# State space scan group by group, with a second stream of projections and Fourier products between its parts

## What is computed

```
p = h @ w_in                                  # x, B, C, step sizes, z, f, gate_f, gate_s
y = scan(x, dt, B, C) both ways + d_skip * x  # 4 groups of 8 heads, chunks of 128 tokens
y_ssd = rmsnorm(y * silu(z), w) @ w_ssd_out
u = fft2(f, tokens and 128 channels).real
y_four = u @ w_four_out
mix = (sigmoid(gate_f) * y_four + sigmoid(gate_s) * y_ssd) @ w_o
```

## Time and profile before

| what | value |
|---|---|
| median of three runs | 3232.49 us |
| profiled execution | 3232.91 us |
| its span, first to last instruction | 3231.3 us |
| mean granted PE clock | 0.957 of full speed |
| PE busy / weight loads | 2991.0 us (93%) / 1603.5 us |
| DVE, ACT, POOL busy | 1119.7, 483.4, 544.1 us |
| mean DMA rate over the span | 224 GB/s |

### The profile page before, as it was taken

The page is one execution under the profiler, slowest core; times in us unless marked ns, Lnnn a source line. Parts: engine busy times, 40 slices in busy tenths (PEclk is TensorE's granted clock), DMA queues, the critical chain, the costliest instruction groups (busy, mean ns, idle before and its releaser), DMA issues.

```text
span 3231.3 us, 39368 instructions
## 1 busy us (share of the span) xinstructions
PE 2991.0 (93%) x16166; PEld 1603.5 (50%) x16166; DVE 1119.7 (35%) x1859; ACT 483.4 (15%) x847; POOL 544.1 (17%) x650
## 2 busy tenths in 40 slices
PE   5998788998799999999999988998999999799996
PEld 2446453857333333333333326877887778433333
DVE  3665562011333333333333323463001446222112
ACT  1111111001110111101010102233001232211111
POOL 0000650000122323232323211021110011000000
PEclk9998788999799999999999999999999999799998
DMA  6344002324299999999999973122443211599991
GB/s 226 116 145 160 1 1 104 129 102 160 108 375 395 396 395 397 394 397 394 397 394 397 395 292 127 53 79 87 145 143 128 105 38 43 186 387 385 386 386 67
DMA packets 334385, 728.08 MB, mean 225 GB/s; under 512 B 17920, under 2 KB 63420, under 8 KB 333932
## 3 DMA queue, kind: packets, MB, share of 16 engines
q1 hardware_dynamic: 321456, 697.22, 58.3%
q0 software_dynamic: 8896, 24.59, 2.1%
q10 hardware_dynamic: 3836, 3.58, 0.4%
HBM read 708.55 MB, written 16.78 MB: 224 GB/s over the span
## 4 chain that ended last, share of the span: by engine, by line
PE 67%; DVE 2%; DMA 2%; ACT 1%; issue 1%; SPq 0%; POOL 0%; POOLq 0%; ACTq 0%; DVEq 0%; PEldq 0%
PE P L705 65%; PE P L708 2%; DVE R L1597 1%; DMA WS<-in_w_gate_up 1%; ACT R L2304 0%; ACT L2304 0%; SPq L626 0%; DMA R<-expert_rows,small 0%; ACT xT L2304 0%; DMA expert_rows<-R 0%; ACT ea L2304 0%; POOL R L2826 0%; DVE R L2295 0%; DVE xT L1603 0%; DVE R L1603 0%
## 5 line engine op out<-in xcount | busy, mean ns | idle before, releaser
L705 PE MATMUL P<-R 128*32 128x512 f32 (+10 forms) x6484 | 1264.4, 493 | 88.0 <-POOL R L2668 30.9
L705 PE MATMUL P<-WS,R 128*64 128x512 f32 (+4 forms) x4456 | 1007.4, 589 | 9.5 <-POOLq L2737 2.8
L705 PEld LDWEIGHTS P<-R 128*32 128x32 f32 (+4 forms) x6484 | 525.6, 145 | 551.5 <-issue 461.7
L705 PEld LDWEIGHTS P<-WS,R 128*64 128x64 f32 (+2 forms) x4456 | 314.7, 129 | 633.7 <-issue 620.2
L2304 ACT ACTIVATE R<-P 128x512 f32<-128x512 f32 (+6 forms) x432 | 224.5, 521 | 2001.7 <-PE P L705 1691.5
L705 PE MATMUL P<-R,WS 128*128 128x256 f32 (+1 forms) x1888 | 504.7, 427 | 10.5 <-DVE R L1600 3.5
L1597 DVE TENSOR_TENSOR R<-P,R 64x512 f32<-64x512 f32 (+3 forms) x260 | 171.8, 661 | 781.9 <-ACT R L2304 478.0
L705 PEld LDWEIGHTS P<-R,WS 128*128 128x128 f32 x1888 | 357.6, 191 | 144.2 <-issue 98.4
L705 PE MATMUL P<-xT,WS 128*128 128x256 f32 (+2 forms) x1728 | 401.1, 385 | 9.5 <-ACT xT L2304 3.5
L705 PEld LDWEIGHTS P<-xT,WS 128*128 128x128 f32 (+2 forms) x1728 | 318.0, 188 | 70.9 <-issue 21.3
L1597 DVE TENSOR_TENSOR R<-R 128x512 f32<-128x512 f32 (+9 forms) x360 | 254.8, 708 | 64.9 <-ACT R L2304 53.0
(11 more groups left out here) (163 smaller groups left out, 985.6 us busy)
## 6 DMA issues: line engine op xcount, KB each, us to landing
WS<-in_w_gate_up SPq DMA_DIRECT2D x192, 1024.0 KB, 11.3
R<-in_w_down SPq DMA_DIRECT2D x128, 1024.0 KB, 12.9
R<-in_w_gate_up SPq DMA_DIRECT2D x64, 1024.0 KB, 14.4
WS<-in_w_in SPq DMA_DIRECT2D x60, 1024.0 KB, 7.5
WS<-in_w_mod SPq DMA_DIRECT2D x24, 1024.0 KB, 7.4
R<-in_moe_w_down SPq DMA_DIRECT2D x23, 1024.0 KB, 8.6
WS<-in_moe_w_gate SPq DMA_DIRECT2D x20, 1024.0 KB, 11.2
WS<-in_moe_w_down SPq DMA_DIRECT2D x17, 1024.0 KB, 8.2
```

The lines of the kernel that those rows point to most:

```text
L705: return nc.tensor.matmul(out, lhsT, rhs, start=start, stop=stop, skip_group_check=True)
```

## The change

The gs, u, z, ff1, ff2 and gf products become one list of 40 items and 256 products (`FRONT`), cut into parts (`PARTS1`); PE's `front(name)` issues a part. Parts stand behind the step sizes, behind the second and fourth decay sum, in each of the 32 scan steps and behind the scan. They use banks P2 and P3 in turn, with semaphores f_done and f_free; ACT empties them, DVE those of z. The scan runs group by group: four steps, both directions in each. `decays` of the next step now stands before the front part in every step, ahead of dg. The products of z with Y (`gate_y`) stand in DVE's queue behind the fourth and sixth step of a group, for the group before. Buffers move: GS into the context half of hT, V_ and UT into x tiles of finished groups, zs and YT into BT, GF into Bf and Cf, U and MX into the place that H left. POOL's Y_init waits for x's transposes only, so it runs in the convolution stage. The transposes of Y come in two halves, before the first and second w_ssd_out unit. The order of weight units follows. Left out below are the removed stage code, index changes of H and the old ACT loops.

```diff
+FRONT = ([("gs", m) for m in range(8)] + [("u", i) for i in range(4)] + [("z", 0), ("z", 1)]
+         + [("f1", f) for f in range(4)] + [("z", 2), ("z", 3)] + [("f1", f) for f in range(4, 8)]
+         + [("z", 4), ("z", 5)] + [("f2", i) for i in range(4)] + [("z", 6), ("z", 7)] + [("gf", m) for m in range(8)])
+FRONT_MM = [(j, k) for j, (kind, _) in enumerate(FRONT) for k in range({"f1": 2, "f2": 4}.get(kind, 8))]
+PARTS1 = ([("dt", 24), ("seg1", 8), ("seg3", 12)]
+          + [((g, q), k) for g, ks in enumerate(([10, 10, 5, 5, 5, 5, 6, 6], [3] * 8, [3] * 8, [3] * 6 + [7, 7]))
+             for q, k in enumerate(ks)]
+          + [("end1", 16), ("end2", 8), ("end3", 56)])
+PART1, _at = {}, 0
+for _n, _k in PARTS1:
+    PART1[_n] = (_at, _at + _k)
+    _at += _k
...
+        zt = reg(SCR, 2, N)
+        zs = [BT[:, :, 512 * i:512 * i + 128] for i in range(2)]
+        YT = reg(12288, 16, N)
+        GS = hT[:, :, 0:N]
+        GF = [Bf[:, t, :] for t in (0, 1, 2, 4, 5, 6)] + [Cf[:, t, :] for t in range(2)]
+        MX = reg(24576, KT, N)
+        U = reg(26624, 2, D)
+        V_ = [XT[:, f % 4, 512 * (f // 4):512 * (f // 4) + 512] for f in range(8)]
+        UT = [XT[:, i, 1024:1536] for i in range(4)]
...
-                  + [proj(w_in, OFF_Z + 512 * i, 512) for i in range(4)]
-                  + [down(a["w_ssd_out"][0], 4 * i, 4) for i in range(4)]
                   + [proj(w_in, OFF_GS + 512 * i, 512) for i in range(2)]
                   + [proj(w_in, OFF_F + 512 * i, 512) for i in range(2)]
+                  + [proj(w_in, OFF_Z + 512 * i, 512) for i in range(4)]
                   + [proj(w_in, OFF_GF + 512 * i, 512) for i in range(2)]
+                  + [down(a["w_ssd_out"][0], 4 * i, 4) for i in range(4)]
                   + [proj(a["w_four_out"][0], 512 * i, 512) for i in range(2)]
                   + [proj(a["w_o"][0], 512 * i, 512) for i in range(2)])
...
-        SSD = [(d, step, ((0, 1, 2, 3), (1, 0, 3, 2))[d][step], g) for d in range(2) for step in range(4) for g in range(4)]
+        SSD = [(d, step, ((0, 1, 2, 3), (1, 0, 3, 2))[d][step], g) for g in range(4) for step in range(4) for d in range(2)]
+        STATES = [(d, step, g) for d, step, c, g in SSD if step < 3]
...
                     unit_used()
                     mod_unit(4 + j // 4)
+            fu = [0]
+            def front(name):
+                for q in range(*PART1[name]):
+                    j, k = FRONT_MM[q]
+                    kind, i = FRONT[j]
+                    if k == 0:
+                        if kind in ("gs", "gf") and i % 4 == 0 or kind in ("u", "z") and i % 2 == 0:
+                            fu[0] = unit()
+                        if j >= 2:
+                            pe.wait_ge(S("f_free"), j - 1)
+                    if k == 1 and j and (FRONT[j - 1][0] in ("gs", "gf") and FRONT[j - 1][1] % 4 == 3
+                                         or FRONT[j - 1][0] in ("u", "z") and FRONT[j - 1][1] % 2 == 1):
+                        pe.wait_ge(S("f_done"), j)
+                        pe.sem_inc(S("unit_used"), 1)
+                    b = P[2 + j % 2]
+                    if kind in ("gs", "gf"):
+                        last = mm(b[:, 0:N], wproj(fu[0], 512, k, 128 * (i % 4), 128 * (i % 4) + 128), hT[:, k, N:2 * N],
+                                  k == 0, k == 7)
+                        end = k == 7
+                    elif kind in ("u", "z"):
+                        c = N + 128 * (i % 2)
+                        last = mm(b[:, :], hT[:, k, c:c + 128], wproj(fu[0], 512, k, 0, 512), k == 0, k == 7)
+                        end = k == 7
+                    elif kind == "f1":
+                        last = mm(b[:, :], U[:, k, 128 * i:128 * i + 128], k1("dft")[:, 512 * k:512 * k + 512], k == 0, k == 1)
+                        end = k == 1
+                    else:
+                        h, t = k // 2, k % 2
+                        last = mm(b[:, 256 * h:256 * h + 256], k1(("dfc", "dfs")[t]), V_[2 * i + h][:, 256 * t:256 * t + 256],
+                                  t == 0, t == 1)
+                        end = k == 3
+                    if end:
+                        last.then_inc(S("f_done"), 1)
+                    if q == len(FRONT_MM) - 1:
+                        pe.wait_ge(S("f_done"), len(FRONT))
+                        pe.sem_inc(S("unit_used"), 1)
             n = unit()
             turn_mod(11)
             b = job("dt", 0)
...
                               k == 0, k == KT - 1)
             done(last)
             unit_used()
+            front("dt")
             pe.wait_ge(S("dA_ready"), 1)
             for c in range(4):
@@ -891,6 +950,8 @@
                     mm(b[:, 64 * q:64 * q + 32], k1(f), dA[:, c, 0:32])
                     last = mm(b[:, 64 * q + 32:64 * q + 64], k1(r), dA[:, c, 32:64])
                 done(last)
+                if c % 2:
+                    front(f"seg{c}")
...
+                if i + 1 < len(SSD) and SSD[i + 1][1] >= 2:
+                    decays(i + 1, nx + 1 if step >= 2 else nx)
+                front((g, i % 8))
                 if step >= 2:
-                    if i + 1 < len(SSD) and SSD[i + 1][1] >= 2:
-                        decays(i + 1, nx + 1)
...
+            for name in ("end1", "end2", "end3"):
+                front(name)
+            pe.wait_ge(S("dg_used"), nx)
+            pe.wait_ge(S("f_free"), len(FRONT))
+            pe.wait_ge(S("mix_step"), 1)
+            for u in range(4):
+                if u < 2:
+                    for i in range(4 * u, 4 * u + 4):
...
+                pe.wait_ge(S("mm_free"), START["ytr"] + 2 * (u + 1))
...
+            eight("four", lambda k: UT[k // 2][:, N * (k % 2):N * (k % 2) + N])
...
             dve.wait_ge(S("Y_init"), 2)
-            for d, step, c, g in SSD:
+            def gate_y(i):
+                g, c, j = i // 2, i % 2, FRONT.index(("z", i))
+                b, four = P[2 + j % 2][:, :].rearrange("p (q n) -> p q n", q=4), zs[i % 2]
+                dve.wait_ge(S("z_sig"), i + 1)
+                tt(four, four, b).then_inc(S("f_free"), 1)
+                dve.wait_ge(S("f_free"), j + 1)
+                yc = Y[:, c, 512 * g:512 * g + 512].rearrange("p (q n) -> p q n", q=4)
+                mark(tt(yc, yc, four), "z_used")
+            for i, (d, step, c, g) in enumerate(SSD):
                 hs = slice(32 * d + 8 * g, 32 * d + 8 * g + 8)
                 yg = Y[:, c - 2, 512 * g:512 * g + 512] if step >= 2 else None
                 if step >= 2:
...
-                F(n, tt(zs[:, i % 2, :], zs[:, i % 2, :], b[:, :]))
-                yc = Y[:, c, 512 * u:512 * u + 512]
-                mark(tt(yc, yc, zs[:, i % 2, :]), "z_used")
+                if g and i % 8 in (3, 5):
+                    gate_y(2 * (g - 1) + (i % 8 == 5))
+            gate_y(6)
+            gate_y(7)
             rooted()
             V(ts(Y[:, 0, :], Y[:, 0, :], st[:, 0:1], None, ALU.mult, ALU.bypass))
             mark(ts(Y[:, 1, :], Y[:, 1, :], st[:, 1:2], None, ALU.mult, ALU.bypass), "mix_step")
...
+            fj = [0]
+            def front(name):
+                q = PART1[name][1]
+                while fj[0] < len(FRONT) and (q == len(FRONT_MM) or FRONT_MM[q][0] > fj[0]):
+                    j = fj[0]
+                    kind, i = FRONT[j]
+                    b = P[2 + j % 2]
+                    fj[0] += 1
+                    act_.wait_ge(S("f_done"), j + 1)
+                    if kind == "z":
+                        if i >= 2:
+                            act_.wait_ge(S("z_used"), i - 1)
+                        mark(fn(zs[i % 2], b[:, :].rearrange("p (q n) -> p q n", q=4), ACT.Sigmoid), "z_sig")
+                        continue
+                    wait(act_, "f_free", j)
+                    if kind == "gs":
+                        ins = fn(GS[:, i, :], b[:, 0:N], ACT.Sigmoid)
+                    elif kind == "gf":
+                        ins = fn(GF[i], b[:, 0:N], ACT.Sigmoid)
+                    elif kind == "u":
+                        ins = fn(U[:, i % 2, 512 * (i // 2):512 * (i // 2) + 512], b[:, :], ACT.Copy)
+                    else:
+                        ins = fn((V_ if kind == "f1" else UT)[i], b[:, :], ACT.Copy)
+                    ins.then_inc(S("f_free"), 1)
+                    act_.wait_ge(S("f_free"), j + 1)
...
+            front("dt")
+                if c % 2:
+                    front(f"seg{c}")
+            nx = 0
+            for i, (d, step, c, g) in enumerate(SSD):
+                if i + 1 < len(SSD) and SSD[i + 1][1] >= 2:
+                    act_.wait_ge(S("seg_done"), nx + 1)
+                    if nx:
+                        act_.wait_ge(S("MT_ready"), nx)
+                    A(fn(EX[:, 0:512], P[5][:, :], ACT.Exp))
+                    mark(fn(EX[:, 512:1024], P[6][:, :], ACT.Exp), "EX_ready")
+                    nx += 1
+                front((g, i % 8))
+
+            front("end1")
+            front("end2")
+            front("end3")
...
```

(34 more changed lines are left out.)

89 lines of the change are left out of this document (15 added, 74 removed).

## The result

The changed kernel takes 3143.57 us (median of 4 runs, 3141.0 to 3146.0) where the kernel before, in the same session, takes 3231.37 (3226.64 to 3234.87): a ratio of 0.9729, 95% interval 0.9712 to 0.9746, some 88 us less. The forecast was 3161, its range 3143 to 3195. The profiled execution took 3141.0 us, its span 3139.4.

A forecast was written before the change was run, and what follows sets the result against it. PE, busy 93% of 3231.3 us, was taken as the bound. Starting w_four_out at 661.7 instead of 735.4 us, less 2.0 for Y_init, saves 71.7: 3232.9 becomes 3161 us, range 3143 to 3195.

The forecast's parts named there:

- step 7: Transposes and w_ssd_out units behind the gf units: 63.5 us, so the w_four_out product starts at 661.7 us.
- step 8: Y_init in the convolution: two POOL products may delay DVE by 0 to 6 us, taken as 2.
- Steps 1 to 3: Step sizes' end (308.9) to scan start (340.2 us): gs matmuls 12.5 and 8.8, decay sums 8.0, half clock 2.0.
- Step 4: PE work in the scan: output steps 89.0, state products alone 14.0, front matmuls 99.7, sum 202.7 us.
- Step 5: Cover in the scan: no other engine is the bound; uncovered waits cost 8.0 us, weight loads at seams 2.
- Step 6: Behind the scan: z6 and z7 14.0 us, then gf units hiding the norm's root 31.3, PE idling 2.6.
- it goes better: Rival, chance 0.09: the uncertain 8.0, seams, clock, Y_init and 2.2 of the sums vanish; 3145 us.
- The holes stay open: Rival, chance 0.12: state product handshakes are paid at all 24 later-group steps, 30 to 42 us; 3191 to 3203.
- Clock: Rival, chance 0.04: many short waits at the seams keep PE at half clock through the scan; 3364 us.
- No effect: Rival, chance 0.03: a load or semaphore order holds the w_four_out product or the experts; 3233 us.

The follow-up runs named there:

- yinit_dt: The changed kernel with POOL's Y_init waiting for the end of the convolution, so it runs under the step size projection; 3141.84 us, ratio 0.9716.
- gate_cb: The changed kernel with the second gate product of a group issued after CBm of the seventh step; 3141.09 us, ratio 0.971.
- lumped: The changed kernel with the same front matmuls given to the scan in blocks rather than three per step; 3196.9 us, ratio 0.9891.
- yinit_late: The changed kernel with POOL's Y_init back behind the decay factors, as before the change; 3157.19 us, one run.
- best: The changed kernel with the edits of yinit_dt and gate_cb, and the square of Y's first half ahead of z7's sigmoid; 3135.64 us, ratio 0.9697.
- gate_early: The changed kernel with the gate product issued before DVE's wait for PE's diagonal part, ahead of the Y addition; 3143.1 us, ratio 0.9716.

## Why the prediction was right, and where its sizes were off

The mechanism was the forecast's: the holes of the state passes, the decay chain and the root take the front matmuls, the clock stays up, and what is left is one wait per group for CBm and one for the root. The time came out 20.2 us lower than forecast (3141.0 against 3161.2, profiled execution to forecast). Of this, 15.2 lie before the w_four_out product (663.7 us, the 661.7 of step 7 and the 2.0 of step 8, against 648.5) and 5.0 in the unchanged rest, which is within the scatter of the runs above. The median of the runs, 3143.57 us, is 0.6 us above the lower end of the range, 3143, and two of the four runs lie under it: that the time fell inside is luck, and the gain was forecast too small, 72 us for 88. By steps:

- *Steps 1 to 3* (31.3 us): measured 27.3, from 313.8 to 341.1. Two rows of the changed kernel's timeline, PE:

```profile
313.88 13.39 PE L724 MATMUL P<-R,WS 128*128 128x256 f32 x48
327.10 2.76 PE L724 MATMUL P<-small,C 128*128 128x32 f32 x24
```

  The page counts each of these matmuls as two records, so the 24 gs took 13.4 where I said 12.5 (12.1 to 12.4 in yinit_dt, gate_cb, lumped, yinit_late and best). The decay sums were the term that I had mis-sized: 12 of the 24 take 2.76 us at full clock, 5.5 in all against my 8.0, just under my lower bound (5.8). The 2.0 for more half clock was not needed beside the cold start. And the wait of 9.7 us for POOL is gone, as forecast.
- *Step 4* (202.7 us of PE work in the scan): measured 195.0 busy. An output step takes 4.72 us from start to start without a state product (2.64 for the product with H and dg, 2.08 for the next decay products), and so 5.58 with one, where I put 5.20 and 5.92. The step of 5.20 held its own gap of 0.31 us and the tail of the matmul ahead of it, 0.16. The step of 5.92 held no idle time and was at clock 1.00, yet 22 merged records of it took 0.4 us longer than the 22 at the same place of a step take in the changed kernel; no run shows why:

```profile
449.24 4.28 PE L705 MATMUL P<-R 128*128 128x64 f32 x22
424.12 3.89 PE L724 MATMUL P<-R 128*128 128x64 f32 x22
```

  (The first row is of the kernel before.) Eight steps of each are 6.6 us. A unit's duration holds its last matmul's tail, so 0.86 us per 512 columns is right for a seam, not 0.873: some 2 us in 132 front matmuls and the states. Some 1 us goes the other way, for the tails ahead of the eight waits are in the busy time.
- *Step 5* (8.0 us of waits, 2.0 of seams): measured 7.1 us of waits, and nothing at the seams. Three waits for CBm of 1.76 us against 1.7 to 2.1; the waits for POOL in the fifth step 0.3 against 0.4; f2 0.7 against 0.5. gate_early and gate_cb show that the gate product in DVE's queue is what makes PE wait. POOL was 80.6 us busy in the scan, DVE 95.3, ACT 50.3, of 202.1: none is the bound. No seam exposes a weight load.
- *Step 6* (14.0 and 31.3 us): measured 13.8 and 31.1, with an idle time of 2.50 us for ACT where I had 2.6, behind three gf units:

```profile
570.03 17.53 PE L724 MATMUL P<-R,WS 128*128 128x256 f32 x80 [2.50 <-ACT R L2337]
588.14 1.94 PE L727 MATMUL P<-C,R 128*128 128x128 f32 x16 [0.57 <-ACT R L2337]
```

- *Step 7* (63.5 us): measured 60.4. I had taken the transposes at the busy time of the earlier trace rows, which was at clock 0.65. At full clock 16 records take 1.94 us, not 3.0: 2.3 us for both halves. The rest is again the unit's tail.
- *Step 8* (2 us, bounds 0 and 6): measured 4.5 (and 0.4 more, since the step size projection took 14.0 us for 13.6), the one term that went the other way. I thought that POOL's first product would fall into DVE's own wait; it does, for 2.5 of its 3.6 us, but its end holds up DVE's scaling (1.36 us for 0.55), and the second product holds up the first tap product until it is done (3.99 us for 0.8). That makes DVE 4.0 us late, 2.4 more than its slack of 1.6; the other 2 us or so are the half clock behind PE's idle time, which I had left out. The Trainium skill (SBUF — State Buffer, "Who interferes with whom") states an exclusive lock between the two engines; the first tap product, which ends only behind POOL's second product, agrees with it. The step as that rule alone would have it was put at 5.6 us, with the whole 7.2 us of POOL on DVE; the measured 4.5 lies between that and my 2.

The errors of steps 1 to 7 add up to 18.1 us in the same direction (4.0, 10.6, 0.4 and 3.1), less 2.9 of step 8. Most of them have one source: durations read from stretches in which PE was partly at half clock (the sums, the transposes) or had gaps (the output steps), used for a stream in which it has neither. Of the signs that I had named, the clock, the waits and their releasers, and the convolution (4.5 us longer, under the 6) came as said. The sizes did not: the scan with its front takes 202 us and not 213, PE's busy time falls by 38 us and not 20, and POOL and DVE are busy for 40 and 47% of the scan and not 50 to 60.

Of the rivals, *it goes better* (3145) is where the time came out, though not for its reason alone: of the 16.2 us that it took away, the waits (8.0) are nearly all there (7.1) and Y_init cost 2.9 more instead of 2.0 less; only the seams, the sums and the 2.0 for the clock went. The prices of the output steps and the transposes, which it left alone, gave the rest, so that its number fits is mostly luck. *The holes stay open* did not happen with three front products per step; lumped shows it happening, and dearer (54 us in the scan) than the 30 to 42 put down, since the cover works in the output steps too. *Clock*: 1.00 over the whole scan. The Trainium skill (TensorE: Matmul & The Clock Gate, "A second HAM failure mode: psum-queue depth-cycling") tells of a kernel whose clock oscillates from short idle times as it cycles through PSUM banks. The two banks of the front show no such thing here, at clock 1.00; idle times of 1 to 2.5 us in the variants are sometimes followed by a single drop. *No effect*: excluded, w_four_out starts 86.9 us earlier.

What stays open: how the gain divides between the places outside the scan (no run has the front there alone), why a step with a state product is 0.4 us shorter now, the price of Y_init's old place in the new kernel (one run, mixed with other drops of the clock), and why the same idle time is sometimes followed by half clock and sometimes not.

## What to carry to other kernels

When a chain of short products with handshakes cannot be made faster, put independent long work into every one of its gaps; here three matmuls of 512 columns at a time were enough, and the same work in blocks kept only 35 us of the 88. Price a dense stream from start to start of neighbours in a full clock stretch, not from a stage's busy time or a unit's duration. And ask of each operation moved to "idle" POOL which DVE instructions it will lie beside: under the step sizes, where DVE has next to nothing to do, these two products cost nothing that the profile shows; in the convolution they cost 4.5 us.

## What was not expected of the hardware

A short idle time of PE can cost more than itself. The granted clock fell to half for some 3 to 4 us behind idles of 1.07 us (best), 1.75 (yinit_dt), 1.76 (yinit_late, twice), 1.97 (gate_early), 2.34 (the convolution of the changed kernel) and 2.50 us (gate_cb). Behind the same idle times it also stayed full: behind 1.07 us in gate_cb, behind 1.76 us three times and 2.50 us once in the changed kernel. The windows of yinit_late behind its wait of 5.16 us, and of best behind 1.07 us, show the drop:

```profile
343.50:347.50 4.00, 4.00 (x8) 2.52 (x9) 0.69 (x1) 0.00 (x0) 1.04 (x1) 0.50 0.00 0
```

```profile
529.00:533.00 4.00, 4.00 (x21) 2.92 (x21) 1.60 (x3) 0.39 (x1) 1.04 (x1) 0.74 0.00 0
```

A drop costs 1 to 2 us here, some 3 behind the wait of 5.16 us. These runs show no rule for when it comes, and it is one reason why the sum of small waits removed is not quite the time gained.

A POOL product of two SBUF tensors can hold up a single DVE operation for nearly its whole length: the first tap product took 3.99 us instead of 0.8 beside a POOL product of 3.68, and the three behind it were not slowed. DVE's multiplication by a per-partition scalar, with one tensor in SBUF as its input, is held up too, in the one place seen: 1.36 us instead of 0.55 in the convolution, in the rows above.
